# A latent-attention query projection regrouped into nope tiles and rotary tiles, with the rotary rows put in place by transfers

## The reference, cut to what matters

```python
c_u, c_v, cq, ckv, kr = jnp.split(h @ o_w_in, O_SPLITS, axis=-1)      # 512, 512, 384, 256, 32 wide
q  = (rmsnorm(cq, q_a_gain) @ w_uq).reshape(b, s, 8, 64 + 32)         # 8 heads: 64 nope + 32 rope columns
kv = (rmsnorm(ckv, kv_a_gain) @ w_ukv).reshape(b, s, 8, 64 + 64)
q_nope = rmsnorm(q[..., :64], q_gain[:64])
q_rope = apply_rope(rmsnorm(q[..., 64:], q_gain[64:]), cos, sin)
k_nope = rmsnorm(k_nope, k_gain[:64]);  k_rope = apply_rope(rmsnorm(kr, k_gain[64:]), cos, sin)
# scores = (q_nope, q_rope) . (k_nope, k_rope) / sqrt(96), chunk-causal softmax, times v
```

## Time and profile before

| | |
|---|---|
| median of 3 runs | 1120.57 us (1119.88 to 1120.65) |
| the profiled execution's own time | 1120.37 us |
| its span, first to last instruction | 1118.6 us |
| PE busy | 1107.2 us, 99% of the span |
| DVE, ACT, POOL busy | 563.9, 421.2, 87.5 us |
| DMA | 105.98 MB, mean 95 GB/s |
| granted TensorE clock | 1.000 |

### The profile page before, as it was taken

The page is one execution under the profiler, slowest core; times in us unless marked ns, Lnnn a source line. Parts: engine busy times, 40 slices in busy tenths (PEclk is TensorE's granted clock), DMA queues, the critical chain, the costliest instruction groups (busy, mean ns, idle before and its releaser), DMA issues. The chain is left out here.

```text
span 1118.6 us, 13557 instructions
## 1 busy us (share of the span) xinstructions
PE 1107.2 (99%) x5059; PEld 887.3 (79%) x5059; DVE 563.9 (50%) x786; ACT 421.2 (38%) x662; POOL 87.5 (8%) x120
## 2 busy tenths in 40 slices
PE   9999999999999999999999999999999999999998
PEld 7777678888888888888877765688888888888887
DVE  6678877434433433242466588665433443443321
ACT  5545445323322322131345567544332332332110
POOL 6000000001100100000102000000100100110000
PEclk9999999999999999999999999999999999999999
DMA  7412213333233333332233200233233333327431
GB/s 240 153 57 76 76 58 112 99 104 99 82 106 94 94 99 101 101 95 84 72 99 95 83 25 1 76 94 105 84 113 94 94 94 95 101 86 169 113 124 46
DMA packets 101144, 105.98 MB, mean 95 GB/s; under 512 B 26219, under 2 KB 77616, under 8 KB 100976
## 3 DMA queue, kind: packets, MB, share of 16 engines
q1 hardware_dynamic: 83392, 103.04, 30.1%
q10 hardware_dynamic: 16656, 2.10, 1.1%
q0 software_dynamic: 1056, 0.30, 0.1%
HBM read 101.23 MB, written 2.10 MB: 92 GB/s over the span
## 5 line engine op out<-in xcount | busy, mean ns | idle before, releaser
L1103 DVE TENSOR_TENSOR w_lo<-raw,w_hi 128x1024 fp32r<-128x1024 f32 (+2 forms) x192 | 224.7, 1176 | 418.2 <-ACT w_hi L678 415.5
L678 ACT ACTIVATE w_hi<-raw 128x1024 fp32r<-128x1024 f32 (+2 forms) x192 | 194.5, 1018 | 468.7 <-PE ps L1666 442.1
L1664 PE MATMUL ps<-h_hi,w_hi 128*128 128x512 f32 x912 | 359.8, 394 | 1.3 <-DVE conv_h L1305 0.7
L1666 PE MATMUL ps<-h_hi,w_lo 128*128 128x512 f32 x912 | 355.1, 389 | 0.0
L1665 PE MATMUL ps<-h_lo,w_hi 128*128 128x512 f32 x912 | 355.0, 389 | 0.0
L1664 PEld LDWEIGHTS ps<-h_hi,w_hi 128*128 128x128 f32 x912 | 171.3, 188 | 43.6 <-issue 6.1
L1665 PEld LDWEIGHTS ps<-h_lo,w_hi 128*128 128x128 f32 x912 | 171.3, 188 | 36.3 <-issue 1.7
L1666 PEld LDWEIGHTS ps<-h_hi,w_lo 128*128 128x128 f32 x912 | 171.2, 188 | 36.0
L589 POOL TENSOR_TENSOR ffn_t<-ffn_t,row_scale 128x512 f32<-128x512 f32 x40 | 50.9, 1294 | 701.3 <-ACT ffn_t L864 701.3
L1664 PE MATMUL ps<-act_hi,w_hi 128*128 (+1 forms) x176 | 68.5, 389 | 0.0
L1665 PE MATMUL ps<-act_lo,w_hi 128*128 (+1 forms) x176 | 68.5, 389 | 0.0
(11 more groups left out here) (286 smaller groups left out, 1168.2 us busy)
## 6 DMA issues: line engine op xcount, KB each, us to landing
raw<-in_w_ffn_in SPq DMA_DIRECT2D x88, 512.0 KB, 3.5
raw<-in_w_ffn_out SPq DMA_DIRECT2D x44, 512.0 KB, 3.8
raw<-in_e_w_in SPq DMA_DIRECT2D x17, 512.0 KB, 3.8
raw<-in_o_w_in SPq DMA_DIRECT2D x8, 512.0 KB, 3.6
raw<-in_o_w_out SPq DMA_DIRECT2D x8, 512.0 KB, 3.6
raw<-in_e_w_out SPq DMA_DIRECT2D x8, 256.0 KB, 3.9
raw<-in_e_w_out SPq DMA_DIRECT2D x4, 512.0 KB, 4.3
out_tok<-x_blocks ACTq DMA_DIRECT2D x16, 128.0 KB, 2.5
```

The lines of the kernel that those rows point to most:

```text
L678: ins = act.activation(dst, src, ACT.Copy)
L1103: ins = TT(dst, src, high, ALU.subtract)
L1664: MM(dst, st_hi, mv_hi, start=start, stop=False)
L1666: return MM(dst, st_lo, mv_hi, start=False, stop=stop)
```

## The change

- The three loads of `w_uq` are now: all 8 heads' rope columns (8 x 32 = 256), the nope columns of heads 0 to 3 (4 x 64 = 256), and those of heads 4 to 7. Six tiles, 54 matmuls. All later loads have a number lower by one, and there are 187. `uq_swap` is gone.
- Banks 4 and 5 hold the rope tiles (32 rows a head, four heads a tile). ACT copies them to a tile `rope` in SBUF. POOL then issues 24 transfers from SBUF to SBUF, three a head, that put the rope rows, and the rope rows with halves swapped, in `o_q`.
- ACT copies each head's 64 nope rows from PSUM to `o_q` (`q_split`). Squares and table products now read `o_q` in SBUF, and the squares wait for the transfers (12 for each round).
- PE: `q_sums` waits for the squares alone, not for the table products. `q_sums(0)` stands one `cu_load` later, `spread(M_OQ)` too. `q_load(3)` is gone. `key_tiles` waits for the copies of `q_split(1)`.
- ACT: root of `M_OQ + 1` ahead of `key_squares(0)`; both halves of the key gains on ACT. DVE: of the second round one table product, then the root of `M_OQ + 1`, then three table products and `yc_gate(2)`, `yc_gate(3)`; no key gains.
- The splits in the attention move: the one at head 2 on ACT is gone, that before `o_pt(6)` on DVE is behind `yd_sum(2)`.
- Some semaphores are joined into others.

```diff
-FFN_IN = (26, 122)
-FFN_OUT = (70, 166)
-O_CQ, O_CKV, O_CV, O_UKV, O_OUT = 92, 96, 100, 112, 114
-O_UQ, O_CU = (104, 105, 110, 111), (106, 107, 108, 109)
-N_LOADS = 188
+FFN_IN = (26, 121)
+FFN_OUT = (70, 165)
+O_CQ, O_CKV, O_CV, O_UKV, O_OUT = 92, 96, 100, 111, 113
+O_UQ, O_CU = (104, 105, 110), (106, 107, 108, 109)
+N_LOADS = 187
@@ SP
-            dst = raw[:, n % 2, 0:768].rearrange("p (k n) -> p k n", k=3)
-            src = o_w_uq[0].rearrange("(k p) n -> p k n", p=P)
-            he, ho = 96 * 2 * j, 96 * (2 * j + 1)
-            sp.dma_start(dst[:, :, 0:96], src[:, :, he:he + 96]).then_inc(raw_landed[n % 2], 16)
-            sp.dma_start(dst[:, :, 128:160], src[:, :, ho + 64:ho + 96]).then_inc(raw_landed[n % 2], 16)
-            sp.dma_start(dst[:, :, 192:256], src[:, :, ho:ho + 64]).then_inc(raw_landed[n % 2], 16)
+            src = o_w_uq[0].rearrange("(k p) (h c) -> p k h c", p=P, c=96)
+            heads, c = ((slice(0, 8), slice(64, 96)), (slice(0, 4), slice(0, 64)), (slice(4, 8), slice(0, 64)))[j]
+            for k in range(3):
+                dst = raw[:, n % 2, 256 * k:256 * k + 256].rearrange("p (h c) -> p h c", h=8 if j == 0 else 4)
+                sp.dma_start(dst, src[:, k, heads, c]).then_inc(raw_landed[n % 2], 16)
@@ POOL
-        uq_swap(0)
-        uq_swap(1)
+        for h in range(HEADS):
+            r, to = 32 * (h % 4), 64 * (1 - h % 2)
+            pool.wait_ge(oq_split, h // 4 + 1)
+            for d, a, n in ((0, 0, 32), (32, 16, 16), (48, 0, 16)):
+                pool.dma_start(o_q[to + d:to + d + n, h, :], rope[r + a:r + a + n, h // 4, :]
+                               ).then_inc(rope_placed[h // 4], 16)
@@ ACT
+        def rope_copy():
+            act.wait_ge(load_used, O_UQ[0] + 1)
             for i in range(2):
-                h = 2 * j + i
+                act.activation(rope[:, i, :], ps[:, 4 + i, :], ACT.Copy).then_inc(oq_split, 1)
+        def q_split(r):
+            act.wait_ge(load_used, O_UQ[1 + r] + 1)
+            for h in range(4 * r, 4 * r + 4):
+                a = 64 * (h % 2)
+                act.activation(o_q[a:a + 64, h, :], ps[a:a + 64, 6 + h // 2 % 2, :], ACT.Copy).then_inc(oq_split, 1)
+        def q_squares(r):
+            act.wait_ge(rope_placed[r], 16 * 12)
+            for h in range(4 * r, 4 * r + 4):
+                act.wait_ge(oq_split, 2 + h + 1)
                 if h >= 4:
                     act.wait_ge(sums_ready, M_OQ + 1)
...
-                act.activation(q_sq(h), ps[:, b0 + i, :], ACT.Square).then_inc(oq_squared, 1)
+                act.activation(q_sq(h), o_q[:, h, :], ACT.Square).then_inc(oq_squared, 1)
...
-        q_squares(0, 4)
+        rope_copy()
         through(104)
-        q_squares(1, 6)
+        q_split(0)
...
         through(106)
+        q_squares(0)
+        through(107)
         rms(M_OQ, ps[:, 4, :], 1)
...
-        q_squares(2, 4)
+        q_split(1)
         through(110)
+        act.wait_ge(u_ready, 4)
         rms_table()
-        q_squares(3, 6)
+        q_squares(1)
         yc_square(0)
         yc_square(1)
+        rms(M_OQ + 1, ps[:, 3, :], 1)
         key_squares(0)
-        rms(M_OQ + 1, ps[:, 3, :], 1)
+        key_gains(0)
         yc_square(2)
         yc_square(3)
         key_squares(1)
-        key_gains_1()
+        key_gains(1)
...
-            if h == 2:
-                through(111)
@@ DVE
-        q_tiles(0, 4)
-        through(104)
-        q_tiles(1, 6)
         through(106)
+        q_tiles(0)
+        through(107)
...
-        q_tiles(2, 4)
         through(110)
...
         yc_gate(0)
         yc_gate(1)
-        q_tiles(3, 6)
+        q_tiles(1, 1)
+        rms(M_OQ + 1, ps[:, 3, :], 1)
+        q_tiles(1, 3, 1)
         yc_gate(2)
         yc_gate(3)
-        key_gains_0()
-        rms(M_OQ + 1, ps[:, 3, :], 1)
@@ PE
-            pe.wait_ge(oq_turned, 4 * r + 4)
+            pe.wait_ge(oq_squared, 4 * r + 4)
...
         cu_load(0)
+        cu_load(1)
+        pe.wait_ge(oq_split, 1)
         q_sums(0, 4)
-        cu_load(1)
+        cu_load(2)
         spread(M_OQ, (4, 5, 6, 7))
-        cu_load(2)
         cu_load(3)
-        pe.wait_ge(oq_scaled, 2)
-        q_load(2, 4)
+        pe.wait_ge(oq_scaled, 4)
+        q_load(2, 6)
...
-        pe.wait_ge(oq_scaled, 4)
-        q_load(3, 6)
...
-            pe.wait_ge(oq_turned, 6 + 2 * half)
+            pe.wait_ge(oq_split, 10)
```

More of the change, by code:

```diff
@@ L203, in program @@
     k_pairs = (at("k_pair_a", [P, 2, S], F32, h_at + 28 * K), at("k_pair_b", [P, 2, S], F32, h_at + 16 * K))
+    rope = at("rope", [P, 2, S], F32, R + 40 * K)
     sq_more = at("sq_more", [P, 2, S], F32, R + 48 * K)
@@ L276, in program @@
     conv_tap_b = sem("conv_tap_b")
-    conv_tap_c = sem("conv_tap_c")
     ea_scaled = sem("ea_scaled")
@@ L331, in program @@
     kr_columns = sem("kr_columns")
-    uq_columns = sem("uq_columns")
+    rope_placed = [sem(f"rope_placed{i}") for i in range(2)]
+    oq_split = sem("oq_split")
     spatial_turned = sem("spatial_turned")
@@ L336, in program @@
     cv_squared = sem("cv_squared")
-    cv_square = sem("cv_square")
     cv_scale = sem("cv_scale")
@@ L345, in program @@
     ok_gained = sem("ok_gained")
-    ok_gained_dve = sem("ok_gained_dve")
     rs_spread = sem("rs_spread")
@@ L605, in _ @@
             ins.then_inc(kr_columns, 1)
[L607 to L615, removed]
-        uq_swap(0)
-        uq_swap(1)
+        for h in range(HEADS):
[4 more added lines that the diff above has]
+                               ).then_inc(rope_placed[h // 4], 16)
         pool.wait_ge(kr_rotated, 1)
-        pool.wait_ge(uq_columns, 2)
         for n, h in enumerate((0, 2, 4, 6, 1, 3, 5, 7)):
@@ L627, in _ @@
         pool.wait_ge(kr_copied, HEADS)
-        uq_swap(2)
-        uq_swap(3)
         scale_silus(1)
@@ L673, in hi @@
                 act.wait_ge(kr_columns, n - O_CKV + 1)
-            if n in O_UQ:
-                act.wait_ge(uq_columns, O_UQ.index(n) + 1)
             pairs = list(zip(ordered(n, w_hi[:, s, :], None), ordered(n, None, raw[:, n % 2, :])))
@@ L944, in _ @@
             act.activation(v_c[:, t, :], ps[:, t, :], ACT.Gelu_apprx_tanh, scale=tiny[:, 6, t:t + 1]).then_inc(cv_ready, 1)
-        def q_squares(j, b0):
-            act.wait_ge(load_used, O_UQ[j] + 1)
+        def rope_copy():
+            act.wait_ge(load_used, O_UQ[0] + 1)
             for i in range(2):
-                h = 2 * j + i
+                act.activation(rope[:, i, :], ps[:, 4 + i, :], ACT.Copy).then_inc(oq_split, 1)
[8 more added lines that the diff above has]
+                act.wait_ge(oq_split, 2 + h + 1)
                 if h >= 4:
@@ L964, in key_squares, with key_gains @@
                 act.activation(k_sq[:, 2 * half + j, :], ps[:, 4 + 2 * half + j, :], ACT.Square).then_inc(ok_squared, 1)
-        def key_gains_1():
+        def key_gains(half):
             for j in range(2):
-                act.wait_ge(ok_squared, 3 + j)
-                act.activation(k_pairs[1][:, j, :], ps[:, 6 + j, :], ACT.Copy, scale=g_col(G_OK)).then_inc(ok_gained, 1)
+                act.wait_ge(ok_squared, 2 * half + j + 1)
+                act.activation(k_pairs[half][:, j, :], ps[:, 4 + 2 * half + j, :], ACT.Copy, scale=g_col(G_OK)
+                               ).then_inc(ok_gained, 1)
         def value_copy(half, part, bank):
@@ L997, in _ @@
         act.activation(tiny[:, 8, 0:4], tiny[:, 7, 0:4], ACT.Abs_reciprocal_sqrt, bias=eps_col[:, :], scale=1.0 / 512
-                       ).then_inc(cv_square, 1)
-        act.wait_ge(cv_square, 1)
+                       ).then_inc(cv_squared, 1)
+        act.wait_ge(cv_squared, QT + 1)
         act.activation(tiny[:, 13, 0:4], tiny[:, 8, 0:4], ACT.Square, scale=float((0.5 / 512) ** 0.5)
-                       ).then_inc(cv_square, 1)
-        through(107)
+                       ).then_inc(cv_squared, 1)
+        through(108)
         gelu_table()
@@ L1065, in _ @@
                 act.activation(yc_hi[:, h - 2, :], yc[:, h - 2, :], ACT.Copy).then_inc(yc_hi_ready, 1)
-            if h == 2:
-                through(111)
             if h == 6:
                 rms_table()
-                through(112)
-        through(113)
+                through(111)
+        through(112)
         o_out(3)
@@ L1296, in tap_c @@
             STT(out=conv_y[:, j, 2:], in0=conv_h[:, j, 0:S - 2], scalar=g_col(G_CONV + j), in1=conv_y[:, j, 2:],
-                op0=ALU.mult, op1=ALU.add).then_inc(conv_tap_c, 1)
+                op0=ALU.mult, op1=ALU.add).then_inc(conv_tap_b, 1)
         through(8)
@@ L1344, in ya_tiles @@
             for j in range(4):
-                dve.wait_ge(conv_tap_c, j + 1)
+                dve.wait_ge(conv_tap_b, 4 + j + 1)
                 TT(conv_y[:, j, :], ps[:, j, :], conv_y[:, j, :], ALU.mult).then_inc(ya_ready, 1)
@@ L1456, in _, with q_tiles @@
         through(O_CV + 3)
-        def q_tiles(j, b0):
-            for i in range(2):
-                h = 2 * j + i
+        def q_tiles(r, count=4, first=0):
```

(18 more changed lines are left out.)

## The result

The median went from 1120.35 us (1119.72 to 1120.89, 13 runs) to **1123.35 us** (1122.16 to 1124.39, 13 runs): a ratio of 1.0026, interval 1.0019 to 1.0033, so slower by 3.0 us. That lies inside the stated range (1118.4 to 1124.0), but 1.1 us above the forecast's own (up to 1122.2), and beside the 1123.5 that was given for the rival "PE slows after its wait". The profiled execution of after took 1123.59 us with a span of 1121.8, so it stands 3.2 us above the one of before, and its rows can be compared with those shown, but for 0.44 us that arose ahead of this stretch (see the part on the prediction).

What follows compares the result with a forecast made beforehand. PE was taken as the only bound, busy 99%. Waits of 5.0 us against 4.08 saved put the keys' sums 0.7 later; less 0.3 in the attention, +0.4 on 1120.57 gave 1121.0 us, stated range 1118.4 to 1124.0.

Steps and rivals of the forecast that it cites:

- PE slows after its wait: Rival: 3.75 us without work slows the keys' sums and value matmuls, +1 to +4, say +2.5 us: 1123.5; chance 0.10.
- The saving: Query loads on PE: 18 matmuls removed at 0.227 us each, at most 4.08 us saved.
- The transfers: POOL, round 0: issues of 0.52 us, landing at 619.2, at worst 620.7, before the 621.2 needed; cost 0.
- Load 104: Rope-column load in 3072 small pieces: ACT's split 0 to 1 us later, 1.6 us of cover, cost 0.
- The three waits: Second round, PE: 0.65 us for bias additions, 0.6 for the root, 3.75 for the keys' squares; 5.0 in all.
- The keys' sums: On PE, to begin at 657.55 against 656.85, 0.7 us later; ends 0 and 1.5.
- the 0.2 us of short gaps: Second round, PE: short gaps of before that the new waits were to take in, 0.2 us.
- The attention: Without the split at head 2, ACT is free 0.28 us earlier: gain 0.3 us, ends 0 and 0.6.
- The step that failed: After the keys' sums: same order, a chain over ACT and DVE, so the 0.7 us delay is carried on unchanged.
- the third rival: The rival "PE slows after its wait": matmuls behind the 3.75 us wait run slower, 1123.5 us; chance 0.10.
- late transfers: Rival: transfers land after 621.2, so PE waits ahead of the first query sums; 3.3 us at worst, 1124.3; chance 0.11.
- one sign of being wrong: Forecast is wrong if matmuls behind PE's wait for the keys' squares start more than 0.23 us apart.

Runs made afterwards that it cites:

- experiment 1: Changed kernel plus 14 unused PE products between the second spread and the keys' sums: 1121.41 us, ratio 1.0008 to the kernel before.
- experiment 8: Changed kernel with ACT's and DVE's lists reordered (keys' squares ahead of yc squares, root behind the table products and one yc gate), PE's list kept: 1119.07 us.
- experiment 6: Kernel before plus six unused ACT squares ahead of the keys' second squares and 14 unused PE products in the wait: 1124.26 us.
- experiment 7: Kernel before plus three unused ACT squares ahead of the keys' second squares: 1122.54 us, ratio 1.0019.
- experiment 3: Changed kernel with the second round's root back behind all table products and yc gates on DVE: 1120.40 us, ratio 0.9999 to the kernel before.
- experiment 2: Changed kernel with the keys' second squares and gains ahead of yc squares 2 and 3 on ACT: 1122.45 us, ratio 1.0017 to the kernel before.
- experiment 5: Kernel before plus six unused ACT squares ahead of the keys' second squares, none of the change: 1125.60 us, ratio 1.0048.
- experiment 4: Changed kernel with round 0's twelve transfers issued twice and the squares waiting for all 24: 1130.93 us, ratio 1.0094 to the kernel before.

## Why the prediction was right in part, and where it failed

- **The saving** is there: 54 query matmuls, 18 fewer records. After's second spread begins at 653.76 where before's began at 655.72.
- **The transfers**: right. ACT's squares follow its split without a wait, `q_sums(0)` starts at 623.95 (forecast 623.4) with no idle, and an issue took 0.49 us (0.58 at most) where I had 0.52:

```profile
620.71 1.14 ACT L955 ACTIVATE sq<-o_q 128x512 f32<-128x512 f32 x2
```

```profile
L609 POOL DMA_DIRECT2D o_q<-rope x24: 487/487/580, 610.6 to 621.8; - x24
...
DMA to landing us min/median/max: 1.8/2.5/4.2
```

- **Load 104**: its split started at 589.01 against 588.26, 0.75 later, within my 0 to 1 and its cover.
- **The three waits**: forecast 0.65, 0.6 and 3.75 us, measured 0.92, 0.74 and 3.81, each at its place and with its releaser. The first was too small because the four half-tile copies took 2.44 us, not 1.94: ACT took 0.61 us for each, with 64 partitions, and 1.10 for the two full copies of the rope tiles, so half the partitions saved nothing. By the prediction's own terms `key_tiles(1)` ends at 651.8, not 652.05, and the second wait is 0.8; the root fixes PE's next start, so the 0.7 us does not change.
- **The keys' sums** were to begin 0.7 us later. They begin 1.86 later (658.71 against 656.85 in the earlier trace rows). Of that, 0.44 arose ahead of the stretch (its first query matmul starts at 604.82, against 604.38 in the earlier trace rows), where PE waited 0.7 us for the program's first input. That wait was 0.2 in the profiled execution of before and 1.4 in experiment 1's: it isn't the change. Leaving it out, 1.4 against 0.7: a term mis-sized by 0.7, within the ends given for it (0 to 1.5). The waits came to 5.5 us where I had 5.0, and 5.5 less the 4.08 saved is already the 1.4: the 0.2 us of short gaps that the new waits were to take in isn't there.
- **The attention** gave back 0.3 us, as forecast: 3.5 us at the spread of the key root (664.63 against 661.11), 3.2 at the end of the span.
- **The step that failed** is "What follows (key root, spread, norms, first scores) has the same order and is a chain over ACT and DVE, so I carry 0.7 on." The order is the same, the speed is not. From the keys' sums to the spread of the key root PE took 5.92 us where it had taken 4.26, with the clock at half for most of it: 1.7 us in the profiled executions, 1.9 between the medians (experiment 1). I had this as the third rival, with the right place, the right mechanism and nearly the right time, and gave it 0.10, with the argument that "nothing before has a wait of this length in the middle of work, so nothing decides it". That argument was no reason for a small chance: the forecast itself made a wait of 3.75 us, and the only rows that showed PE behind a pause, had it slow (with a granted clock of 1.00 there, so whether that was the same thing is open). By the Trainium skill, "TensorE: Matmul & The Clock Gate" (Part 1), an idle engine drops to 1.2 GHz; the trace agrees, with 0.50 granted from 656.0 to 662.8 us.

Together, in medians: order +1.4, clock +1.9, attention -0.3, measured +3.0. The forecast mechanism held, and the rival came on top of it; I had treated the two as alternatives.

That the time lies inside the stated range is in part luck. The range reached 1124.0 for late transfers, which did not come; the forecast's own range ended at 1122.2. That range was also added up wrongly: its ends, -0.9 and +1.1 on 1121.0, give 1120.1 to 1122.1, not 1119.6 to 1122.2. By the prediction's own line for slower, 1122.8, the outcome was slower, which had 0.19 against 0.64 for same. And one sign of being wrong could not have fired on the value matmuls: "more than 0.23 us apart" is the spacing of matmuls 512 wide, and these, half as wide, start 0.12 us apart at the full clock and 0.21 at half.

## What to carry to other kernels

Time taken from the engine that bounds the kernel arrives only as far as the ordered lists of the other engines let it: write out, instant by instant, when each thing that it waits for is ready, and order those lists by who waits, as experiment 8 did. A new wait on TensorE of about 2 us or more can cost, beyond its length, slower matmuls behind it (here 0.7 to 1.9 us); forecast both as one case. Where such a wait can't be removed, matmuls of no use in it are worth trying: here 14 of them made the kernel 1.9 us faster.

## What the runs showed of the hardware

- The longer PE's longest wait in this stretch, the more often the granted clock fell, and by chance from run to run. The wait is read from the profiled execution of each kernel, the fall from each run's clock over the span.

| longest wait of PE in the stretch | kernel | runs with a fall | cost where it fell |
|---|---|---|---|
| up to 1.3 us | experiments 1, 6 and 8 | 0 of 28 | |
| 1.9 us | experiment 7 | 4 of 11 | 0.7 us |
| 2.3 us | experiment 3 | 9 of 11 | 1.0 us |
| 2.6 us | experiment 2 | 8 of 11 | 1.9 us |
| 3.8 us | after, experiment 5 | 18 of 18 | 1.9 and 1.3 us |
| 4.6 us, and 3.8 | experiment 4 | 4 of 4 | not separated |

- The fall did not come at a fixed point of the wait: 1.1 us after its start in after, 0.5 us after its end in experiment 5, 1.5 us after its end in experiment 3. The trace of after has waits of 0.92 and 0.74 us ahead of the long one, that of experiment 5 has none; what such short waits and the small matmuls between them add to the odds was not tested apart.

- POOL's copies and DVE slow each other: the key copies took 6.82 us beside DVE's table products (5.65 in the earlier trace rows), and those products and the two splits behind them 3.86 and 2.11 us. With POOL idle, three such products took 2.08 us (at 653.74 above), so four some 2.8, and the same two splits 1.29 (at 631.96). PE waited for neither:

```profile
622.38 6.82 POOL L617 COPY o_k<-kr 64x512 f32<-64x512 f32 x8
```

```profile
621.71 3.86 DVE L1465 SCALAR_TENSOR_TENSOR o_q<-o_q,gains,tables 128x512 f32<-128x512 f32 x4
625.49 2.11 DVE L1106 TENSOR_TENSOR w_lo<-raw,w_hi 128x512 fp32r<-128x512 f32 x2
```
